# A chain of ten swiglu layers: each weight transfer of gate and up carries all eight feature chunks of one matrix instead of four chunks of both

## The chip, the core and the metric

One core of one Trainium2 chip runs the whole program. TensorE (PE) multiplies, ScalarE (ACT) and VectorE (DVE) work elementwise, and SyncE's queue (SP) starts every weight transfer. The metric is the device time of one execution in microseconds (us), lower is better.

## The reference, cut to what matters

Three model blocks follow each other on 256 tokens of width 1024, in float32. They hold ten swiglu layers, which the change touches, with mixers (delta rule, latent attention, state space, gating, pooling) between them:

```python
D_MODEL, SEQ, D_FF = 1024, 256, 2816
def swiglu(x, w_gu, w_down):
    gate, up = jnp.split(x @ w_gu, 2, axis=-1)
    return (jax.nn.silu(gate) * up) @ w_down
...
x = x + 0.5 * swiglu(rms_norm(x, ffn1_norm[l]), ffn1_w_gu[l], ffn1_w_down[l])
```

Eight of the ten layers normalize their input with a learned gain; two (in the second block) have no gain and no root mean square ahead of them.

## The kernel before

Every product is made of three float32r passes: a weight tile is split into a rounded part (`weights_hi`) and a rest (`weights_lo`), the input likewise (`input_hi`, `input_lo`), and TensorE adds hi x hi, hi x lo and lo x hi. Weights come as **items** of up to 1 MB. The plan of all items is written once, in order (`plan_ffn`, `plan_columns`, `plan_rows`), and five slots of SBUF hold them in turn. For each item, SP loads the raw weights into a slot once TensorE has used the item five places earlier (`load_weights`, L186); ACT rounds them (`round_weights`, L198), with the gain of each chunk of 128 features as its scale, so that an item with a gain takes one instruction for each chunk (L210) and one without takes one in all (L206); DVE writes the rest over the raw weights (`split_weights`, L215; L228 with a gain, L223 without). ACT and DVE are at most `LEAD` = 3 items ahead of TensorE. They run in order, and DVE starts an item after ACT has finished all of it.

A swiglu layer (`ffn`, L791) walks the 2816 hidden features in 11 steps of 256. In step s TensorE takes item a(s), which holds feature chunks 0 to 3 of the gate's 256 columns and of up's 256 columns, then item b(s) with chunks 4 to 7 of both, then the 256 rows of the down matrix of step s-1. So it goes gate, up, gate, up, 24 matmuls each, and then 24 wide ones. ACT and DVE in step s: round and split a(s)+3, scale the gate (L895), round and split b(s)+3, silu (L873), hidden = silu x up (L903), rounded hidden (L878), rest of it (L906), and round and split the item three places past the down item.

The last two down items are taken by `last_rows` (L292) in quarters of the output, so that the residual sum (L323, L325) and the transposes for the next layer's input (`turn`, L352; L360) can start before the end. Quarters come "by halves": the first two hold features 0 to 511 (chunks 0 to 3) of all tokens, the last two hold 512 to 1023 (chunks 4 to 7). ACT and DVE turn each into `input_hi` (L370) and `input_lo` (L385). In the first step `before_chunk` (L445) makes TensorE wait for the quarters that a chunk needs, and `sum_row` (L426, L430) sums the row of inverse roots that L895 multiplies with.

Between stages that are not joined stands a barrier (L150): all engines end their stage before any starts the next.

Of the kernel before, what the change touches and what calls it, by code (L numbers as in the profile page):

```python
# [13 lines left out]
P = 128  # L14
D = 1024
T = 256
NT = T // P
DC = D // P
FF = 2816
FSTEP = 256  # L20
# [72 lines left out]
class Core:  # L93
# [78 lines left out]

    def halves(self, gate, up, g0, u0, k0, gain):
        parts = [(slice(j * FSTEP, (j + 1) * FSTEP), w[k0 * P:(k0 + 4) * P, c0:c0 + FSTEP].rearrange("(k p) n -> p k n", p=P))
                 for j, (w, c0) in enumerate(((gate, g0), (up, u0)))]
        self.items.append((parts, 4, 2 * FSTEP, None if gain is None else (gain, k0)))
# [450 lines left out]
def plan_ffn(K, gate, up, g0, u0, down, gain):  # L627
    for s in range(NF):
        for k0 in (0, 4):
            K.halves(gate, up, g0 + s * FSTEP, u0 + s * FSTEP, k0, gain)  # L630
        if s:
            K.rows(down, (s - 1) * FSTEP, 2)
    K.rows(down, (NF - 1) * FSTEP, 2)
# [157 lines left out]
def ffn(K, feed, tail, alpha=1.0, join=True):  # L791
    nc, norm = K.nc, feed.norm
    gated, gscaled, silued, hidden, hrounded, hsplit = (K.count_of(s) for s in (
        "gate_ready", "gate_scaled", "gate_silued", "hidden_ready", "hidden_rounded", "hidden_split"))
    LAST = NF - 1
    with ExitStack() as e:
# [4 lines left out]
        with K.stage(3 * NF, join=join) as (block, n0):  # L801
# [14 lines left out]
            def _(pe):  # L816
                def part(bank, n, c0, w0, before=None):
                    wh, wl = K.item(n)
                    for m in range(2):
                        o, ms = bank[:, m * T:(m + 1) * T], slice(w0 + m * P, w0 + (m + 1) * P)  # L820
                        for k in range(4):
                            if before and m == 0:
                                before(pe, c0 + k)
                            c = c0 + k
                            nc.tensor.matmul(o, wh[:, k, ms], K.hi[:, c, :], start=(c == 0 and m == 0), stop=False,  # L825
                                             skip_group_check=True)
                            nc.tensor.matmul(o, wh[:, k, ms], K.lo[:, c, :], start=False, stop=False, skip_group_check=True)  # L827
                            last = nc.tensor.matmul(o, wl[:, k, ms], K.hi[:, c, :], start=False, stop=(c == DC - 1),  # L828
                                                    skip_group_check=True)
                    return last  # L830

# [1626 lines left out]
```

## Time and profile before

| what | before |
|---|---|
| median of 3 runs | 3296.45 us (3295.63 to 3297.97) |
| the profiled execution, its time and span | 3295.09 us, 3293.3 us |
| TensorE matmuls busy | 2952.7 us, 90% |
| DVE, ACT busy | 1847.4 us (56%), 1441.7 us (44%) |
| granted TensorE clock over the span | 0.931 |

Busy matmuls overlap, so 90% is not the share of peak. What decides is where TensorE stands still, and what it then waits for.

### The profile page before, as it was taken

The numbers are of one execution on the slowest core, as the hardware profiler recorded it, in microseconds if no ns is written. First come the engines' busy times: TensorE is split into PE (matmuls) and PEld (weight loads), VectorE is DVE, ScalarE is ACT, GpSimd is POOL, SyncE is SP. The second block draws the span as 40 slices with busy tenths as digits, with TensorE's granted clock in tenths as the row PEclk, the third lists the DMA queues.
The fourth block names the chain that finished last, engine by engine and source line by source line (L and its number), as shares of the span: only waits on it lengthen the run. The fifth ranks groups of instructions, "written<-read, shape, count | busy, mean of one in ns | idle before, by whom it ended". The sixth has DMA issues, their size and how long they took to land. (4 is left out here: it accounts for less than half of the span.)

```text
span 3293.3 us, 48031 instructions
## 1 busy us (share of the span) xinstructions
PE 2952.7 (90%) x20618; PEld 2734.3 (83%) x20618; DVE 1847.4 (56%) x2513; ACT 1441.7 (44%) x1925; POOL 16.3 (0%) x21
## 2 busy tenths in 40 slices
PE   4998788996997999999897698999999799999799
PEld 4998686996995699898797597898999699999698
DVE  3558464654554565545557635556554565655655
ACT  3544212544443454443434343344444354544543
POOL 0000000000000000000000100000000000000000
PEclk8999786998997899999998798999999899999899
DMA  4554100553552255555254043554555355554454
GB/s 160 180 191 155 64 1 26 185 188 112 179 190 94 71 192 192 168 191 165 91 167 143 1 154 117 177 192 154 192 185 161 123 183 192 179 192 141 167 189 138
DMA packets 371959, 489.30 MB, mean 149 GB/s; under 512 B 17103, under 2 KB 331044, under 8 KB 371620
## 3 DMA queue, kind: packets, MB, share of 16 engines
q1 hardware_dynamic: 371410, 486.11, 45.5%
q8 instruction: 163, 2.67, 0.3%
q14 instruction: 48, 0.39, 0.0%
q10 hardware_dynamic: 338, 0.13, 0.0%
HBM read 485.14 MB, written 1.05 MB: 148 GB/s over the span
## 5 line engine op out<-in xcount | busy, mean ns | idle before, releaser
L825 PE MATMUL work<-input_hi,weights_hi 128*128 128x256 f32 x3520 | 989.4, 281 | 8.8 <-PEq L150 6.8
L827 PE MATMUL work<-input_lo,weights_hi 128*128 128x256 f32 x3520 | 986.2, 280 | 0.0
L828 PE MATMUL work<-input_hi,weights_lo 128*128 128x256 f32 x3520 | 985.8, 280 | 0.0
L223 DVE TENSOR_TENSOR weights_lo<-weights_raw,weights_hi 128x2048 fp32r<-128x2048 f32 (+2 forms) x282 | 629.3, 2236 | 451.6 <-ACT weights_hi L206 451.3
L825 PEld LDWEIGHTS work<-input_hi,weights_hi 128*128 128x128 f32 x3520 | 666.6, 189 | 13.7 <-DVE weights_lo L228 6.9
L827 PEld LDWEIGHTS work<-input_lo,weights_hi 128*128 128x128 f32 x3520 | 666.9, 189 | 3.7
L828 PEld LDWEIGHTS work<-input_hi,weights_lo 128*128 128x128 f32 x3520 | 666.4, 189 | 0.0
L210 ACT ACTIVATE weights_hi<-weights_raw,params 128x512 fp32r<-128x512 f32 (+1 forms) x736 | 462.1, 701 | 363.8 <-DMA weights_raw<-in_ffn_w_in 177.0
L228 DVE SCALAR_TENSOR_TENSOR weights_lo<-weights_raw,params,weights_hi 128x512 fp32r<-128x512 f32 (+1 forms) x736 | 493.1, 733 | 224.7 <-ACT weights_hi L210 224.6
L206 ACT ACTIVATE weights_hi<-weights_raw 128x2048 fp32r<-128x2048 f32 (+2 forms) x282 | 524.6, 1862 | 173.0 <-DMA weights_raw<-in_ffn_w_up 106.2
L253 PE MATMUL work<-input_hi,weights_hi 128*128 128x256 f32 (+2 forms) x1160 | 333.2, 287 | 42.4 <-PEq L150 26.5
L286 PE MATMUL acc<-weights_hi,hidden_hi 128*128 128x512 f32 x880 | 344.7, 392 | 1.0 <-DVE hidden_lo L906 1.0
L287 PE MATMUL acc<-weights_lo,hidden_hi 128*128 128x512 f32 x880 | 343.6, 390 | 0.0
L288 PE MATMUL acc<-weights_hi,hidden_lo 128*128 128x512 f32 x880 | 342.7, 389 | 0.0
L254 PE MATMUL work<-input_lo,weights_hi 128*128 128x256 f32 (+2 forms) x1160 | 329.2, 284 | 0.0
L255 PE MATMUL work<-input_hi,weights_lo 128*128 128x256 f32 (+2 forms) x1160 | 329.1, 284 | 0.0
L253 PEld LDWEIGHTS work<-input_hi,weights_hi 128*128 128x128 f32 (+2 forms) x1160 | 221.5, 191 | 45.2 <-issue 41.9
L254 PEld LDWEIGHTS work<-input_lo,weights_hi 128*128 128x128 f32 (+2 forms) x1160 | 221.6, 191 | 0.7
L255 PEld LDWEIGHTS work<-input_hi,weights_lo 128*128 128x128 f32 (+2 forms) x1160 | 221.3, 191 | 0.5
L878 ACT ACTIVATE hidden_hi<-hidden 128x512 fp32r<-128x512 f32 x110 | 69.5, 632 | 292.7 <-DVE hidden L903 292.7
L895 DVE TENSOR_TENSOR gate_r<-work,inverse_root 128x512 f32<-128x512 f32 x88 | 60.8, 690 | 241.5 <-PE work L828 241.5
L288 PEld LDWEIGHTS acc<-weights_hi,hidden_lo 128*128 128x128 f32 x880 | 165.2, 188 | 35.5
(407 smaller groups left out, 3239.3 us busy)
## 6 DMA issues: line engine op xcount, KB each, us to landing
weights_raw<-in_ffn_w_gu SPq DMA_DIRECT2D x176, 512.0 KB, 4.7
weights_raw<-in_ffn_w_in SPq DMA_DIRECT2D x176, 512.0 KB, 4.6
weights_raw<-in_ffn_w_down SPq DMA_DIRECT2D x66, 1024.0 KB, 4.9
weights_raw<-in_w_in SPq DMA_DIRECT2D x44, 1024.0 KB, 5.1
weights_raw<-in_ffn_w_out SPq DMA_DIRECT2D x44, 1024.0 KB, 4.8
weights_raw<-in_a_w_in SPq DMA_DIRECT2D x29, 1024.0 KB, 5.5
weights_raw<-in_ffn_w_gate SPq DMA_DIRECT2D x44, 512.0 KB, 3.7
weights_raw<-in_ffn_w_up SPq DMA_DIRECT2D x44, 512.0 KB, 4.7
```

What stands on the lines that cost most here:

```text
L206: last = self.nc.scalar.activation(self.wh[:, n % SLOTS, 0:kc * cols], raw, ACT.Copy)
L210: last = self.nc.scalar.activation(hi[:, k, :], raw[:, k * cols:(k + 1) * cols], ACT.Copy, scale=g[:, gain[1] + k:gain[1] + k + 1])
L223: last = self.nc.vector.tensor_tensor(self.wl[:, n % SLOTS, 0:kc * cols], raw, self.wh[:, n % SLOTS, 0:kc * cols].bitcast(F32), ALU.subtract)
L228: last = self.nc.vector.scalar_tensor_tensor(out=lo[:, k, :], in0=raw[:, k * cols:(k + 1) * cols], scalar=g[:, gain[1] + k:gain[1] + k + 1 ...
L253: self.nc.tensor.matmul(o, wh[:, k, ms], hi[:, k, :], start=clear, stop=False, skip_group_check=True)
L254: self.nc.tensor.matmul(o, wh[:, k, ms], lo[:, k, :], start=False, stop=False, skip_group_check=True)
L255: last = self.nc.tensor.matmul(o, wl[:, k, ms], hi[:, k, :], start=False, stop=(k == kc - 1), skip_group_check=True)
L286: self.nc.tensor.matmul(o, hi[:, k, ts], wh[:, k, cols], start=(first and k == 0), stop=False, skip_group_check=True)
L288: last = self.nc.tensor.matmul(o, lo[:, k, ts], wh[:, k, cols], start=False, stop=(end and k == kc - 1), skip_group_check=True)
L825: nc.tensor.matmul(o, wh[:, k, ms], K.hi[:, c, :], start=(c == 0 and m == 0), stop=False, skip_group_check=True)
L827: nc.tensor.matmul(o, wh[:, k, ms], K.lo[:, c, :], start=False, stop=False, skip_group_check=True)
L828: last = nc.tensor.matmul(o, wl[:, k, ms], K.hi[:, c, :], start=False, stop=(c == DC - 1), skip_group_check=True)
```

## The change

An item of gate or up now holds all eight chunks of the 256 columns of one matrix, [128, 8, 256], in one transfer. Before, it held four chunks of both matrices, [128, 4, 512], in two transfers. Item a(s) is the gate's and item b(s) is up's. The number and size of items stay as they are. TensorE uses the helper `project` (L237), which takes an item's 48 matmuls; given `before`, it takes chunks 0 to 3 of both column halves and then chunks 4 to 7. The semaphore `gate_ready` goes; its waiters now wait until item a(s) is used.

```diff
-    def halves(self, gate, up, g0, u0, k0, gain):
-        parts = [(slice(j * FSTEP, (j + 1) * FSTEP), w[k0 * P:(k0 + 4) * P, c0:c0 + FSTEP].rearrange("(k p) n -> p k n", p=P))
-                 for j, (w, c0) in enumerate(((gate, g0), (up, u0)))]
-        self.items.append((parts, 4, 2 * FSTEP, None if gain is None else (gain, k0)))
...
     for s in range(NF):
-        for k0 in (0, 4):
-            K.halves(gate, up, g0 + s * FSTEP, u0 + s * FSTEP, k0, gain)
+        for w, c0 in ((gate, g0), (up, u0)):
+            K.columns(w, c0 + s * FSTEP, FSTEP, DC, gain)
...
                 for s in range(NF):
-                    before = feed.before_chunk if s == 0 else None
-                    K.arrived(pe, a_item(s))
                     if s >= 2:
                         pe.wait_ge(*(gscaled if norm else silued)(s - 1))
-                    part(gate_bank(s), a_item(s), 0, 0, before)
+                    K.project(pe, a_item(s), gate_bank(s), (K.hi, K.lo),
+                              (lambda k: feed.before_chunk(pe, k)) if s == 0 else None)
+                    if s == 0:
+                        feed.sum_row(pe)
                     if s >= 2:
                         pe.wait_ge(*hidden(s - 1))
-                    part(up_bank(s), a_item(s), 0, FSTEP).then_inc(K.used, 1)
-                    if s == 0:
-                        feed.sum_row(pe)
-                    K.arrived(pe, b_item(s))
-                    part(gate_bank(s), b_item(s), 4, 0, before).then_inc(*gated.up())
-                    part(up_bank(s), b_item(s), 4, FSTEP).then_inc(K.used, 1)
+                    K.project(pe, b_item(s), up_bank(s), (K.hi, K.lo))
...
-                        act.wait_ge(*gated(s + 1))
+                        act.wait_ge(K.used, a_item(s) + 1)
...
-                        dve.wait_ge(*gated(s + 1))
+                        dve.wait_ge(K.used, a_item(s) + 1)
```

On ACT, this is the stage of the latent keys, just ahead of the barrier to the third swiglu layer, whose first three items are rounded there; before:

```order
L210 ACTIVATE weights_hi<-weights_raw,params 128x512 x4
L1888 ACTIVATE k_nope<-work 128x512
L1891 ACTIVATE v_mla<-work 128x2x256
L210 ACTIVATE weights_hi<-weights_raw,params 128x512 x4
L1888 ACTIVATE k_nope<-work 128x512
L1891 ACTIVATE v_mla<-work 128x2x256
L210 ACTIVATE weights_hi<-weights_raw,params 128x512 x4
L150 UNCONDITIONAL_BRANCH
```

and with the change:

```order
L205 ACTIVATE weights_hi<-weights_raw,params 128x256 x8
L1864 ACTIVATE k_nope<-work 128x512
L1867 ACTIVATE v_mla<-work 128x2x256
L205 ACTIVATE weights_hi<-weights_raw,params 128x256 x8
L1864 ACTIVATE k_nope<-work 128x512
L1867 ACTIVATE v_mla<-work 128x2x256
L205 ACTIVATE weights_hi<-weights_raw,params 128x256 x8
L150 UNCONDITIONAL_BRANCH
```

The order is the same, and each of the three items takes eight instructions of 256 columns where it took four of 512.

On DVE, this is the end of the output projection ahead of the second swiglu layer: the last weight split, then the residual sums (L325) that the transposes wait for. Before:

```order
L603 TENSOR_TENSOR input_lo<-h,input_hi 128x256 x8
L223 TENSOR_TENSOR weights_lo<-weights_raw,weights_hi 128x2048
L228 SCALAR_TENSOR_TENSOR weights_lo<-weights_raw,params,weights_hi 128x512 x8
L325 SCALAR_TENSOR_TENSOR x<-x,acc 128x512 x2
L385 TENSOR_TENSOR input_lo<-work,input_hi 128x4x128 x2
L325 SCALAR_TENSOR_TENSOR x<-x,acc 128x512 x2
```

and with the change (L320 is the same sum):

```order
L598 TENSOR_TENSOR input_lo<-h,input_hi 128x256 x8
L218 TENSOR_TENSOR weights_lo<-weights_raw,weights_hi 128x2048
L223 SCALAR_TENSOR_TENSOR weights_lo<-weights_raw,params,weights_hi 128x256 x16
L320 SCALAR_TENSOR_TENSOR x<-x,acc 128x512 x2
L380 TENSOR_TENSOR input_lo<-work,input_hi 128x4x128 x2
L320 SCALAR_TENSOR_TENSOR x<-x,acc 128x512 x2
```

Here too the order is kept, and sixteen short instructions stand ahead of the sums in place of eight.

On TensorE, this is the first step of the second swiglu layer; rows show the semaphores waited for. Before, chunk 4 comes only with item b:

```order
L825 MATMUL work<-input_hi,weights_hi 128x256
L827 MATMUL work<-input_lo,weights_hi 128x256
L828 MATMUL work<-input_hi,weights_lo 128x256
L430 MATMUL acc<-root_diagonals,const 128x256 [waits input_diagonal]
L825 MATMUL work<-input_hi,weights_hi 128x256 [waits input_split,weights_split]
L827 MATMUL work<-input_lo,weights_hi 128x256
```

and with the change, the wait for the second half of the input stands 24 matmuls earlier, in the middle of item a:

```order
L248 MATMUL work<-input_hi,weights_hi 128x256
L249 MATMUL work<-input_lo,weights_hi 128x256
L250 MATMUL work<-input_hi,weights_lo 128x256
L248 MATMUL work<-input_hi,weights_hi 128x256 [waits input_split]
L249 MATMUL work<-input_lo,weights_hi 128x256
L250 MATMUL work<-input_hi,weights_lo 128x256
```

The wait for `input_split` that stood with item b's first matmul, behind 48 matmuls, now stands behind 24.

## Rows read from the trace of the kernel before

**Rows 1.** Windows, first of eight steady stretches: time, PE, PEld, DVE, ACT, clock; and their sum.

```profile
107.00:240.00 133.00, 133.00 (x960) 125.40 (x959) 77.81 (x97) 65.51 (x88) 0.00 (x0) 1.00 0.59 190
...
sum 969.00, PE 969.00 PEld 912.47 DVE 561.44 ACT 476.83 POOL 0.00; mean PE 121.12 PEld 114.06 DVE 70.18 ACT 59.60 POOL 0.00
```

**Rows 2.** Groups by line and shape, the whole trace: the weight instructions of ACT and DVE.

```profile
L210 ACT ACTIVATE weights_hi<-weights_raw,params 128x512 fp32r<-128x512 f32 x704 | 450.2, 712 | 355.7 <-DMA weights_raw<-in_ffn_w_in 177.0 <-DMA weights_raw<-in_ffn_w_gu 175.7 <-PEq L150 3.1
...
L228 DVE SCALAR_TENSOR_TENSOR weights_lo<-weights_raw,params,weights_hi 128x512 fp32r<-128x512 f32 x704 | 481.7, 747 | 224.7 <-ACT weights_hi L210 224.6
```

**Rows 3.** Timeline (start, us): items of eight 128x256 pieces, latent key projection.

```profile
750.20 3.31 ACT L210 ACTIVATE weights_hi<-weights_raw,params 128x256 fp32r<-128x256 f32 x8 [4.29 <-DMA weights_raw<-in_w_dkv]
...
753.55 3.26 DVE L228 SCALAR_TENSOR_TENSOR weights_lo<-weights_raw,params,weights_hi 128x256 fp32r<-128x256 f32 x8
```

**Rows 4.** Timeline of ACT and DVE, one steady step of layer 3.

```profile
851.16 2.56 ACT L210 ACTIVATE weights_hi<-weights_raw,params 128x512 fp32r<-128x512 f32 x4 [2.30 <-DMA weights_raw<-in_ffn_w_gu]
...
856.16 2.57 ACT L210 ACTIVATE weights_hi<-weights_raw,params 128x512 fp32r<-128x512 f32 x4 [2.44 <-DMA weights_raw<-in_ffn_w_gu]
...
862.40 0.68 DVE L903 TENSOR_TENSOR hidden<-silu,work 128x512 f32<-128x512 f32 x1
...
879.06 0.68 DVE L903 TENSOR_TENSOR hidden<-silu,work 128x512 f32<-128x512 f32 x1
```

**Rows 5.** Timeline around the barrier ahead of the memory values.

```profile
47.51 2.54 ACT L210 ACTIVATE weights_hi<-weights_raw,params 128x512 fp32r<-128x512 f32 x4
...
50.09 2.74 DVE L228 SCALAR_TENSOR_TENSOR weights_lo<-weights_raw,params,weights_hi 128x512 fp32r<-128x512 f32 x4 [3.14 <-ACT weights_hi L210]
...
53.15 0.55 PE L1116 MATMUL work<-weights_hi,input_hi 128*128 128x256 f32 x1 [6.93 <-PEq L150]
```

**Rows 6.** Timeline around the barrier ahead of the first layer's input.

```profile
69.43 2.74 DVE L228 SCALAR_TENSOR_TENSOR weights_lo<-weights_raw,params,weights_hi 128x512 fp32r<-128x512 f32 x4 [2.93 <-ACT weights_hi L210]
...
72.88 0.45 PE L360 MATMUL work<-const,x 128*128 128x128 f32 x1 [6.80 <-PEq L150]
```

**Rows 7.** Timeline around the barrier ahead of layer 3.

```profile
810.05 0.60 ACT L1888 ACTIVATE k_nope<-work 128x512 f32<-128x512 f32 x1 [0.58 <-PE work L1875]
...
814.17 0.60 ACT L1888 ACTIVATE k_nope<-work 128x512 f32<-128x512 f32 x1 [0.60 <-PE work L1875]
...
815.14 2.55 ACT L210 ACTIVATE weights_hi<-weights_raw,params 128x512 fp32r<-128x512 f32 x4
...
817.72 2.74 DVE L228 SCALAR_TENSOR_TENSOR weights_lo<-weights_raw,params,weights_hi 128x512 fp32r<-128x512 f32 x4 [1.37 <-ACT weights_hi L210]
...
820.96 0.55 PE L825 MATMUL work<-input_hi,weights_hi 128*128 128x256 f32 x1 [6.83 <-PEq L150]
```

**Rows 8.** Timeline, end of the output projection ahead of layer 2.

```profile
571.86 2.74 DVE L228 SCALAR_TENSOR_TENSOR weights_lo<-weights_raw,params,weights_hi 128x512 fp32r<-128x512 f32 x4 [7.10 <-ACT weights_hi L210]
...
574.63 1.28 DVE L325 SCALAR_TENSOR_TENSOR x<-x,acc 128x512 f32<-128x512 f32 x2
...
576.27 0.60 PE L360 MATMUL work<-const,x 128*128 128x128 f32 x4
```

**Rows 9.** Timeline, first step of layer 2: last quarter's split, and a later matmul.

```profile
583.74 0.69 DVE L385 TENSOR_TENSOR input_lo<-work,input_hi 128x512 fp32r<-128x512 f32 x1 [0.45 <-ACT input_hi L370]
...
585.02 0.28 PE L825 MATMUL work<-input_hi,weights_hi 128*128 128x256 f32 x1
```

**Rows 10.** Page, part 6: issues, KB each, median us to landing.

```profile
weights_raw<-in_ffn_w_in SPq DMA_DIRECT2D x176, 512.0 KB, 4.6
...
weights_raw<-in_w_in SPq DMA_DIRECT2D x44, 1024.0 KB, 5.1
```

**Rows 11.** Waits of TensorE within layers, whole trace, and one in time.

```profile
PE work L825 <- DVE input_lo L385: 2.0, 3, 0.7
...
758.94 0.47 PE L286 MATMUL acc<-weights_hi,hidden_hi 128*128 128x512 f32 x1 [0.52 <-DVE hidden_lo L906]
```

**Rows 12.** Window behind the barrier ahead of layer 3: granted clock before the DMA share.

```profile
820.90:827.00 6.10, 6.04 (x39) 6.07 (x40) 2.74 (x4) 5.50 (x6) 0.00 (x0) 0.73 0.00 0
```

More of the change, by code:

```diff
@@ L792, in ffn @@
     nc, norm = K.nc, feed.norm
-    gated, gscaled, silued, hidden, hrounded, hsplit = (K.count_of(s) for s in (
-        "gate_ready", "gate_scaled", "gate_silued", "hidden_ready", "hidden_rounded", "hidden_split"))
+    gscaled, silued, hidden, hrounded, hsplit = (K.count_of(s) for s in (
+        "gate_scaled", "gate_silued", "hidden_ready", "hidden_rounded", "hidden_split"))
     LAST = NF - 1
@@ L816, in _ @@
             def _(pe):
[L817 to L830, printed above, removed]
                 def pair(s):
```

## Prediction

> **What bounds the kernel now.** I read first the windows of steady stretches inside the swiglu layers, to see whether TensorE ever stands still there. It does not: in eight such stretches of 969 us together its matmuls cover all 969 us and the granted clock is 1.00, while DVE is busy for 561 us (58%) and ACT for 477 us (49%) [rows 1]. One step takes 879.06 - 862.40 = 16.66 us [rows 4]. So inside the layers TensorE's own 120 matmuls a step set the time, and their number, shapes and operands do not change. Then I read the list of TensorE's waits, to see where it stands still elsewhere: at barriers between stages, and at transposes and inputs. A change of the weight items can only act there, or by making ACT and DVE so slow that they fall behind in the steps.
>
> **The cost of an item on ACT and DVE.** The trace already has the new form: in the latent key projection an item with a gain is eight pieces of 256 columns, and takes 3.31 us on ACT and 3.26 us on DVE [rows 3], against 2.56 and 2.74 us for four pieces of 512 [rows 4, 5]. That is +0.75 us on ACT and +0.52 us on DVE for each item. The eight layers with a gain have 704 / 4 = 176 such items [rows 2]: ACT gets 132 us more work, DVE 92 us. The two layers without a gain take one instruction for each item in either form, so 44 items stay as they are.
>
> The Trainium skill ("VectorE: DVE Perf Modes", the section on the TRN2 errata) says that operations from SBUF pay a fixed extra cost for each instruction and advises tiles of at least 512 elements; the change goes from 512 to 256. The trace agrees on the direction. By the page's ScalarE figure of 224 cycles at 1.2 GHz, four more instructions cost 0.75 us, an estimate that is equal to the row; the sum would be the same. The page does not say whether the cost is hidden; that is decided below.
>
> **Inside a step it is hidden.** ACT's first weight item of a step began at 851.16 because its transfer had landed then, and the second at 856.16 for the same reason [rows 4]. With 3.31 us each ACT ends at 854.5 and 859.5, DVE ends the second at 859.5 + 3.3 = 862.8, and the hidden product starts there instead of at 862.40, 0.4 us later. TensorE asks for the result a whole step later, after the next up product. The longest chain of the two engines in a step is: first round 3.3, its split 3.3 and the scaled gate 0.7 (beside the second round), second split 3.3, hidden 0.7, its rounding 0.6, and the round of the down item 1.9, 13.8 us of 16.66. So it does not build up: price 0. If that cover were gone, each microsecond over 16.66 would count 80 times or so. The gate is complete after 48 matmuls of a step instead of 72, so DVE's scaling can come 2.8 us sooner; nobody on the path waits for it, price 0.
>
> **Where it is not hidden: three barriers.** At three places ACT rounds and DVE splits an item of a coming layer as the last act of a stage, and the barrier lets TensorE go only behind it.
> - Ahead of the memory values ACT starts at 47.51, DVE at 50.09 and ends at 52.83, and TensorE starts at 53.15 after 6.93 us of idle time at the barrier [rows 5]. No transfer is waited for. Cost: 0.75 + 0.52 = 1.27 us.
> - Ahead of the first layer's input DVE ends at 72.17 and TensorE starts at 72.88, again after 6.80 us [rows 6]. Cost: 1.27 us.
> - Ahead of layer 3 three items are rounded in turn with the copies of k_nope and v_mla between. ACT idled 0.58 and 0.60 us ahead of the second and third copy, which takes up part: 3 x 0.75 - 0.58 - 0.60 = 1.07 us, and DVE's last split adds 0.52. DVE's end goes from 820.46 to 822.05, and TensorE's start at 820.96 follows [rows 7]. Cost: 1.6 us.
> Together 4.1 us. Lower bound 0, if something else than DVE holds the barriers; upper bound 4.1 plus what the clock does (below).
>
> **Four ends of output projections.** There DVE splits the second item of the next layer and then does the residual sums for the first transposes. Ahead of layer 2 the split at 571.86 was DVE's wait for ACT, and the sums start right behind it at 574.63; the first is done after half of 1.28 us, at 575.3, and TensorE transposes at 576.27 [rows 8], 0.96 us of room. The split moves by 1.27 us, so the transpose is late by about 0.3 us. Ahead of layers 4, 8 and 10 the pattern is the same, with slightly more room: I take 0.9 us for the four, bounds 0 and 4 x 0.35 = 1.4.
>
> **The earlier wait for the second half of the input.** In the first step TensorE needed features 512 to 1023 after 48 matmuls, and now needs them after 24. Layer 2's last quarter is split at 583.74 + 0.69 = 584.43, and the 25th matmul starts at 585.02 [rows 9]: 0.6 us to spare. ACT's and DVE's work between the last transpose and that split is not weight work, so it moves along with TensorE. The whole trace has only 2.0 us of TensorE's waits for this input in the layers, three of them [rows 11]. Price 0.
>
> **Transfers.** 440 issues of 512 KB become 220 of 1024 KB, with the same 1 KB runs. A half lands 4.6 us after its own issue, and the second is issued behind the first; a single 1024 KB item of just the new shape (in_w_in) lands in 5.1 us [rows 10], 0.5 us more, which the dropped second issue about makes up. Price 0, bounds -0.5 to +0.4 us a transfer, which ACT's waits inside the steps take up.
>
> **Ends of layers.** At the end of two layers TensorE waited about half a microsecond for the rest of the last hidden product (0.52 us at 758.94) [rows 11]. The earlier gate can give back up to 1.0 us of that, and slower splits can add up to 0.5 us at others; I take 0.
>
> **The sum** is 4.1 + 0.9 = 5.0 us. The profiled execution took 3295.09 us, so 3300.1 us for one like it; the median of the runs shown is 1.4 us above it, and I predict 3296.45 + 5.0 = 3301.4 us, 0.15% more. Changes within 0.2% (6.6 us, up to 3303.0) are about what a measurement cannot tell from no change, and the forecast lies there, near the edge.
>
> **The rivals.**
> - Slower by more than 0.2%, by the clock. The three barriers' idle times grow from 6.9 to about 8.3 us. Behind the barrier ahead of layer 3 the granted clock averages 0.73 over 6.1 us [rows 12]: 3.3 us at 1.2 GHz, or 1.65 us lost. If each of the three low stretches doubled, 3 x 1.65 = 5 us come on top: 3306. For it: these stretches exist. Against it: they depend on how the start falls, and may as well shorten. Chance 0.15; it decides from 1.6 us of added cost on.
> - Slower by the second half of the input: if the last quarter were more than 0.6 us later, five starts (layers 2, 4, 8, 9, 10) each lose the excess, for 1.3 us of delay 0.7 us each, 3.5 us: 3305. Against it: the quarter hangs on TensorE's transposes, not on weights, except in layer 9. Chance 0.1.
> - Much slower: ACT and DVE fall behind in the steps of 16.66 us, because some wait that I take as loose is tight. One microsecond in each of 80 steps would give 3380. Rows 1 and the 13.8 us speak against it. Chance 0.04.
> - Not slower at all: something other than DVE's split ends the barriers, or transfers land earlier and give the 0.9 us back. Then 3296.5 to 3297.5. Chance 0.13.
> - Faster by more than 0.2%: fuller transfers speed up the whole. TensorE would need 6.6 us of waits for weights inside the layers to win; apart from the barriers, the rows have 2.0 us for inputs and about 1.0 for the hidden product [rows 11]. Chance 0.04. The Trainium skill ("DMA: Bandwidth & Descriptors", the rules for kernel authors) advises transfers of at least 1 MB, which speaks for this one; by that rule alone, with nobody waiting, the time would stay at 3296.5.
> - My forecast, 3298.5 to 3303.5: chance 0.54.
>
> **Range and chances.** 3296.5 to 3306.5 leaves out the far case and the ends of the clock's. Slower by over 0.2%: the clock 0.13, the input 0.09, the far case 0.04 and the forecast's own upper edge 0.06, 0.32 together. Faster by over 0.2%: 0.04. Within: 0.64.
>
> **What would show it.** In the profile after: ACT's and DVE's weight groups at 1408 pieces with a mean near 0.5 us; ACT busy 1574 us, DVE 1939 us; TensorE's three starts behind the barriers 1.3, 2.5 and (with the transposes ahead of layer 2) about 4.5 us later than before; steady windows with TensorE at 100%; a step still 16.66 us; no wait for `input_lo` near the 25th matmul. The prediction is wrong if steps are longer than 16.7 us, if the starts do not move, or if the low-clock stretches change in length.

## The result and the profile after

| | before | after |
|---|---|---|
| median of 20 runs each | 3296.32 us (3292.25 to 3298.87) | 3303.08 us (3296.61 to 3308.07) |
| ratio after / before | | 1.002, 95% interval 1.0013 to 1.0027 |
| profiled execution, its time and span | 3295.09 us, 3293.3 us | 3301.61 us, 3299.8 us |
| TensorE matmuls busy | 2952.7 us | 2953.4 us |
| DVE, ACT busy | 1847.4, 1441.7 us | 1937.0, 1562.4 us |

The change costs 0.2%, 4.3 to 8.9 us by the interval, at the edge of what can be told from no change. The forecast was +5.0 us, 3301.4 us. The median rose by 6.8 us. Between the two profiled executions the span grew by 6.5 us. ACT got 120.7 us more work and DVE 89.6 us, and TensorE, which has the longest list of work, is busy for the same time.

The page after, its busy times, two costly groups and two of the issues (they answer to [rows 2] and [rows 10]; the groups here hold 32 pieces that are not of gate and up):

```profile
PE 2953.4 (90%) x20618; PEld 2734.9 (83%) x20618; DVE 1937.0 (59%) x3217; ACT 1562.4 (47%) x2629; POOL 16.7 (1%) x21
...
L223 DVE SCALAR_TENSOR_TENSOR weights_lo<-weights_raw,params,weights_hi 128x256 fp32r<-128x256 f32 x1440 | 584.6, 478 | 360.2 <-ACT weights_hi L205 360.2
L205 ACT ACTIVATE weights_hi<-weights_raw,params 128x256 fp32r<-128x256 f32 x1440 | 592.8, 495 | 263.8 <-DMA weights_raw<-in_ffn_w_in 128.1
...
weights_raw<-in_ffn_w_gu SPq DMA_DIRECT2D x88, 1024.0 KB, 5.1
weights_raw<-in_w_in SPq DMA_DIRECT2D x44, 1024.0 KB, 5.2
```

A piece takes half a microsecond where one of twice the size took 0.71 to 0.75, so ACT and DVE pay for twice as many instructions. Inside the layers nobody notices. Windows after (columns as in [rows 1]) and, behind them, two hidden products of layer 3 on DVE that are four steps apart:

```profile
107.00:240.00 133.00, 133.00 (x960) 125.40 (x959) 88.88 (x168) 76.98 (x154) 0.00 (x0) 1.00 0.58 190
860.00:980.00 120.00, 120.00 (x871) 113.28 (x871) 77.17 (x146) 68.05 (x137) 0.00 (x0) 1.00 0.59 192
```

```profile
869.73 0.68 DVE L879 TENSOR_TENSOR hidden<-silu,work 128x512 f32<-128x512 f32 x1
...
936.35 0.69 DVE L879 TENSOR_TENSOR hidden<-silu,work 128x512 f32<-128x512 f32 x1
```

TensorE is covered to 100% at a granted clock of 1.00, with DVE at 88.88 us of 133 where it had 77.81, and a step takes (936.35 - 869.73) / 4 = 16.66 us as before. The time is lost at single places. TensorE's rows behind the three barriers, timeline after, to be laid beside [rows 5 to 7]:

```profile
54.64 0.55 PE L1092 MATMUL work<-weights_hi,input_hi 128*128 128x256 f32 x1 [8.19 <-PEq L150]
...
76.68 1.94 PE L355 MATMUL work<-const,x 128*128 128x128 f32 x8 [8.06 <-PEq L150]
...
828.59 0.55 PE L248 MATMUL work<-input_hi,weights_hi 128*128 128x256 f32 x1 [8.11 <-PEq L150]
```

The idle times were 6.93, 6.80 and 6.83 us: +1.26, +1.26 and +1.28, 3.8 us together. I then laid TensorE's instructions of both traces side by side, in their order, and looked where the distance between equal instructions changes. Besides the barriers it does so in two ways.

One is waits. At the end of layer 2 TensorE waits 0.20 us for the hidden product where it waited 0.52 [rows 11]. At the end of layer 3 and in the output projection of the pool mixer ahead of layer 10 it waits longer. After:

```profile
997.99 2.11 ACT L205 ACTIVATE weights_hi<-weights_raw,params 128x256 fp32r<-128x256 f32 x5 [5.50 <-DMA weights_raw<-in_b_w_in]
...
1006.72 0.47 PE L281 MATMUL acc<-weights_hi,hidden_hi 128*128 128x512 f32 x1 [1.45 <-DVE hidden_lo L882]
...
3075.88 1.91 ACT L201 ACTIVATE weights_hi<-weights_raw 128x2048 fp32r<-128x2048 f32 x1 [1.45 <-DMA weights_raw<-in_b_w_out]
...
3081.95 0.80 PE L281 MATMUL acc<-weights_hi,input_hi 128*128 128x512 f32 x1 [10.64 <-DVE input_lo L598]
```

The two waits of TensorE were 0.48 and 8.79 us before, so +0.97 and +1.85 us. Each time ACT had stood waiting for a transfer that the change does not touch (`in_b_w_in`, `in_b_w_out`).

The traces of the experiments e1 to e11, which the next section tells one by one, set these two places apart. At the end of layer 3 the long wait comes back in each of the two other traces that have the changed items and their short instructions in all steps: 1.69 us in e3 and 1.47 in e4. Their transfer of `in_b_w_in` landed 6.85 and 6.63 us after its issue, and 6.61 in the changed kernel. The wait is 0.48 to 0.49 us in the kernel before, e1, e5, e6 and e7, and 0.00 to 0.29 us in e2, e9, e10 and e11, and in all nine the transfer landed after 5.0 to 5.5 us. (In e8, with instructions of 128 columns, it is 2.44 us with a landing of 5.1.) So this 1 us belongs to the change, although why the transfer lands later is open. At the pool mixer the wait goes from 8.69 to 9.82 us in the seven traces with the old items and from 9.30 to 10.67 in the four with new ones in all steps. The ranges overlap, so one pair of traces cannot say how much of the 1.85 us is the change's.

The other way is the clock. The same two matmuls of the latent keys' stage, ahead of the third barrier, before and then after:

```profile
804.17 0.27 PE L1874 MATMUL work<-weights_lo,latent_hi 128*128 128x128 f32 x1
...
807.72 0.28 PE L1875 MATMUL work<-weights_hi,latent_lo 128*128 128x128 f32 x1
```

```profile
807.22 0.41 PE L1850 MATMUL work<-weights_lo,latent_hi 128*128 128x128 f32 x1
...
813.83 0.41 PE L1851 MATMUL work<-weights_hi,latent_lo 128*128 128x128 f32 x1
```

They are 3.55 us apart before and 6.61 us after, and over the whole stage the trace after loses 3.8 us. Windows over that stage (column 8 is the granted clock), before and after:

```profile
796.00:823.00 27.00, 17.37 (x119) 16.43 (x120) 10.15 (x17) 13.53 (x24) 0.00 (x0) 0.75 0.36 118
```

```profile
798.00:831.00 33.00, 21.51 (x121) 20.61 (x122) 11.69 (x29) 15.98 (x39) 0.00 (x0) 0.60 0.29 96
```

A mean of 0.75 over 27 us is 13.5 us at 1.2 GHz, 0.60 over 33 us is 26.4 us. Between 1030 and 1953 us of the trace before, the trace after wins 4.3 us back, all but 0.5 us of it without a shorter wait. Over the whole span the granted clock is 0.931 and 0.930.

Behind the first barrier the clock is lower, too. The 15 us from TensorE's start, before and then after:

```profile
53.15:68.15 15.00, 12.93 (x96) 12.73 (x96) 2.74 (x4) 5.31 (x11) 0.00 (x0) 0.90 0.28 81
```

```profile
54.64:69.64 15.00, 13.99 (x96) 13.79 (x96) 2.59 (x7) 5.00 (x13) 0.00 (x0) 0.82 0.22 70
```

The same 96 matmuls take about 1.0 us more. This repeats: in the four traces in which TensorE idles 8.19 us at that barrier (after, e1, e3, e6) these 15 us have 0.80 to 0.82, in the three with 6.93 us (before, e2, e7) 0.89 to 0.90, and in the three with 1.70 us (e4, e5, e11) 1.00. With 5.83 us (e9, e10) it is 0.86. Behind the second barrier the clock is 0.76 before and after, and behind the third 0.89 and 0.91.

### The profile page after: what moved, and what is told of

Same layout as the page of the kernel before. It is cut to its first block and busy times, and to the rows that moved or that the text cites. A ratio compares the mean times of both kernels' runs of the same rounds, so it can differ in the third digit from the quotient of the medians.

```text
span 3299.8 us, 49309 instructions
## 1 busy us (share of the span) xinstructions
PE 2953.4 (90%) x20618; PEld 2734.9 (83%) x20618; DVE 1937.0 (59%) x3217; ACT 1562.4 (47%) x2629; POOL 16.7 (1%) x21
## 5 line engine op out<-in xcount | busy, mean ns | idle before, releaser
L248 PE MATMUL work<-input_hi,weights_hi 128*128 128x256 f32 (+1 forms) x4680 | 1321.7, 282 | 52.5 <-PEq L150 34.6
L249 PE MATMUL work<-input_lo,weights_hi 128*128 128x256 f32 (+1 forms) x4680 | 1314.6, 281 | 0.0
L250 PE MATMUL work<-input_hi,weights_lo 128*128 128x256 f32 (+1 forms) x4680 | 1313.9, 281 | 0.0
L248 PEld LDWEIGHTS work<-input_hi,weights_hi 128*128 128x128 f32 (+1 forms) x4680 | 887.7, 190 | 59.9 <-issue 41.7
L249 PEld LDWEIGHTS work<-input_lo,weights_hi 128*128 128x128 f32 (+1 forms) x4680 | 887.9, 190 | 4.3
L250 PEld LDWEIGHTS work<-input_hi,weights_lo 128*128 128x128 f32 (+1 forms) x4680 | 887.2, 190 | 0.4
L223 DVE SCALAR_TENSOR_TENSOR weights_lo<-weights_raw,params,weights_hi 128x256 fp32r<-128x256 f32 x1440 | 584.6, 478 | 360.2 <-ACT weights_hi L205 360.2
L205 ACT ACTIVATE weights_hi<-weights_raw,params 128x256 fp32r<-128x256 f32 x1440 | 592.8, 495 | 263.8 <-DMA weights_raw<-in_ffn_w_in 128.1
L281 PEld LDWEIGHTS acc<-weights_hi,hidden_hi 128*128 128x128 f32 x880 | 165.3, 188 | 34.5 <-issue 3.3
L282 PEld LDWEIGHTS acc<-weights_lo,hidden_hi 128*128 128x128 f32 x880 | 165.2, 188 | 30.2
L1092 PE MATMUL work<-weights_hi,input_hi 128*128 128x256 f32 x224 | 65.9, 294 | 19.1 <-PEq L150 19.1
```

What stands on the lines that cost most here:

```text
L205: last = self.nc.scalar.activation(hi[:, k, :], raw[:, k * cols:(k + 1) * cols], ACT.Copy, scale=g[:, gain[1] + k:gain[1] + k + 1])
L223: last = self.nc.vector.scalar_tensor_tensor(out=lo[:, k, :], in0=raw[:, k * cols:(k + 1) * cols], scalar=g[:, gain[1] + k:gain[1] + k + 1 ...
L248: self.nc.tensor.matmul(o, wh[:, k, ms], hi[:, k, :], start=clear, stop=False, skip_group_check=True)
L249: self.nc.tensor.matmul(o, wh[:, k, ms], lo[:, k, :], start=False, stop=False, skip_group_check=True)
L250: last = self.nc.tensor.matmul(o, wl[:, k, ms], hi[:, k, :], start=False, stop=(k == kc - 1), skip_group_check=True)
L281: self.nc.tensor.matmul(o, hi[:, k, ts], wh[:, k, cols], start=(first and k == 0), stop=False, skip_group_check=True)
```

## The experiments

Every kernel was timed in rounds with the kernel before on the same chip, and the ratio is to that.

| kernel | median, us | ratio (95%) |
|---|---|---|
| e1 short instructions alone | 3306.19 | 1.0032 (1.002 to 1.0043) |
| e2 first two steps in the old form | 3296.15 | 1.0002 (0.9993 to 1.0011) |
| e3 two transfers for each item | 3301.20 | 1.0017 (1.0009 to 1.0026) |
| e4 change, with hold | 3283.40 | 0.9962 (0.9948 to 0.9976) |
| e5 before, with hold | 3276.88 | 0.9947 (0.9933 to 0.996) |
| e6 five items ahead of barriers | 3303.99 | 1.0023 (1.0013 to 1.0032) |
| e7 items at projections, 128 columns | 3310.82 | 1.0045 (1.0032 to 1.0058) |
| e8 all items, 128 columns | 3385.35 | 1.0277 (1.0259 to 1.0295) |
| e9 before, one instruction an item | 3296.62 | 1.0003 (0.9994 to 1.0012) |
| e10 after, one instruction an item | 3298.08 | 1.0007 (0.9998 to 1.0016) |
| e11 mixed items, with hold | 3281.75 | 0.9954 (0.9941 to 0.9967) |

The median of the kernel before was 3297.34 us beside e1 to e4, 3295.17 beside e5 to e8 and 3296.29 beside e9 to e11.

**Short instructions or new transfers (e1, e3).** e1 is the kernel before with the pieces cut in two, on ACT and likewise on DVE:

```diff
-                    last = self.nc.scalar.activation(hi[:, k, :], raw[:, k * cols:(k + 1) * cols], ACT.Copy,
-                                                     scale=g[:, gain[1] + k:gain[1] + k + 1])
+                    for c in range(0, cols, 256):
+                        e = min(c + 256, cols)
+                        last = self.nc.scalar.activation(hi[:, k, c:e], raw[:, k * cols + c:k * cols + e], ACT.Copy,
+                                                         scale=g[:, gain[1] + k:gain[1] + k + 1])
```

> The kernel before, items, transfers and TensorE's order unchanged; only ACT and DVE take each item with a gain in eight pieces of 256 columns instead of four of 512. Theory 1 (the cost is the 0.75 us of ACT and 0.52 us of DVE that each item takes longer, where a barrier or a transpose waits for it): +4.1 us at the three barriers and about +0.9 at the four projections, 3301 to 3303 us, as the changed kernel. Rival 2 (single transfers of 1024 KB or the landing of items cost the time): nothing, 3296 us. Rival 3 (gate first, then up, with the earlier wait for the second half of the input costs it): nothing, 3296 us.

e3 is the changed kernel with two transfers of four chunks each:

```diff
-                sp.dma_start(self.raw_item(n).rearrange("p (k n) -> p k n", k=kc)[:, :, cols], src).then_inc(*landed.up(16))
+                dst = self.raw_item(n).rearrange("p (k n) -> p k n", k=kc)[:, :, cols]
+                for k0 in ((0, 4) if n in self.two else (0,)):
+                    ks = slice(k0, k0 + 4) if n in self.two else slice(0, kc)
+                    sp.dma_start(dst[:, ks, :], src[:, ks, :]).then_inc(*landed.up(16))
```

> The changed kernel, but each item of gate and up is loaded by two transfers of 512 KB (chunks 0 to 3, then 4 to 7). Theory 1: the transfers are not on the path, 3303 us as the changed kernel. Rival 2 (the single transfer lands later or disturbs others): back to 3297 us or half of the way.

e1 loses 0.32% with the transfers and TensorE's order of before; e3 loses what the change loses. The number of instructions is enough for the loss, and one transfer or two makes no difference to the total that these runs can tell. e1's time of 3306.19 us is above its expected 3301 to 3303, and its ratio gives 10.5 us. Its trace has the three barriers (+3.8 us) and the four projections (+1.1 us) as expected, and besides them an attention stage behind layer 3 at a low clock, like e6 below.

**Which items (e2, e6, e7).** e2 is the changed kernel, but the items of steps 0 and 1 of each layer are four chunks of both matrices again (`halves` for `s < 2`), with TensorE's order of before in these steps.

> The changed kernel, but steps 0 and 1 of every swiglu layer keep the old items (four chunks of both matrices) and the old order; steps 2 to 10 are as changed. Theory 1: all places where the items' longer work is exposed handle items of steps 0 and 1 alone, so the loss goes, 3296 to 3297.5 us. Rival 2 (transfers): 9 of 11 steps still have single transfers, so about 9/11 of the loss stays, 3301.8 us. Rival 3 (order): the early wait for the input lies in step 0 and goes too, 3296 us, with e1 telling it from theory 1.

The loss is gone, with nine of eleven steps in the new form, and in its trace the idle times at the barriers are back at 6.93, 6.80 and 6.80 us. e2 restores instructions, transfers and order of the first two steps together; that it is the instructions follows from e1. e6 goes the other way, with 256-column pieces for five items alone:

```diff
+            if (gain, s, k0) in (("ffn1_0", 0, 0), ("ffn1_0", 1, 0), ("ffn1_1", 0, 0), ("ffn1_1", 0, 4), ("ffn1_1", 1, 0)):
+                K.short.add(len(K.items) - 1)
```

> The kernel before, with smaller instructions of 256 columns (eight where there were four) on five items alone: the two of layer 1 and the three of layer 3 that stand ahead of the three barriers. All other items, the transfers and TensorE's order stay. Theory: three barriers late by 1.3, 1.3 and 1.6 us, 4.1 to 4.5 us together, 3301.5, with the clock's stretches adding or taking up to 2 us. Rival (the loss is spread over all layers, or comes from the gate's order): within 1 us of the kernel before, 3297 to 3298.

TensorE behind the three barriers in e6:

```profile
54.59 0.55 PE L1126 MATMUL work<-weights_hi,input_hi 128*128 128x256 f32 x1 [8.19 <-PEq L150]
...
76.62 1.94 PE L368 MATMUL work<-const,x 128*128 128x128 f32 x8 [8.05 <-PEq L150]
...
826.07 0.55 PE L835 MATMUL work<-input_hi,weights_hi 128*128 128x256 f32 x1 [8.14 <-PEq L150]
```

The three idle times are those of the changed kernel to 0.03 us. These 20 more instructions on each of two engines cost as much at the barriers as 704 do. But the total was 7.6 us by the ratio (4.3 to 10.5), not 4.1 to 4.5. In the attention behind layer 3 the windows of before and of e6 show where its trace lost the most besides, by the clock:

```profile
1080.00:1116.00 36.00, 29.45 (x116) 18.74 (x116) 23.02 (x63) 16.63 (x46) 0.00 (x0) 0.83 0.00 1
```

```profile
1085.00:1128.00 43.00, 37.42 (x118) 23.18 (x118) 23.11 (x63) 16.14 (x46) 0.00 (x0) 0.66 0.00 1
```

The same work takes about 7 us more at a mean clock of 0.66; 5.7 us come back between 1110 and 1950 us of the trace before. e7 puts pieces of 128 columns on the first three items of layers 2, 4, 8 and 10, which stand at the ends of projections.

> The kernel before, with the first three items of layers 2, 4, 8 and 10 in instructions of 128 columns (sixteen where there were four): ACT takes 2.2 us more for each, DVE 1.6 us. This is three times the dose of the change, at the ends of the four projections alone. Theory (the splits there stand ahead of the residual sums, with 0.96 us of room): the second split ends 3.8 us later or more, and the transposes come 2.8 us late or more at each of the four places, 11 us together or more: 3308 to 3315. If the loss there is linear and has no room at all, the change itself would have cost more than 1 us at each of the four. Rival (the sums were waiting for TensorE's quarters anyway, so the splits are covered): under 3 us, 3297 to 3300.

```profile
579.43 0.90 PE L368 MATMUL work<-const,x 128*128 128x128 f32 x3 [2.74 <-DVE x L333]
```

That is layer 2's first transpose in e7 (idle before it in brackets); the three others wait 2.72, 2.72 and 2.70 us. Predicted was 3.8 - 0.96 = 2.8. Four times 2.72 are 10.9 us, and by the ratio the time rose by 14.8 us (10.5 to 19.1), again more than the waits, as in e6. The room of 0.96 us is real. Whether the change itself uses it up is seen in e1 and after. The transfers, ACT's item, DVE's sum and the transpose, first in e1 and then in the changed kernel:

```profile
566.26 16.00 SPq L194 DMA_DIRECT2D weights_raw<-in_ffn_w_gu  x6
571.89 3.31 ACT L212 ACTIVATE weights_hi<-weights_raw,params 128x256 fp32r<-128x256 f32 x8 [5.22 <-DMA weights_raw<-in_ffn_w_gu]
578.52 1.29 DVE L330 SCALAR_TENSOR_TENSOR x<-x,acc 128x512 f32<-128x512 f32 x2
579.27 0.66 PE L365 MATMUL work<-const,x 128*128 128x128 f32 x4 [0.44 <-DVE x L330]
```

```profile
566.11 14.94 SPq L189 DMA_DIRECT2D weights_raw<-in_ffn_w_gu  x3
571.21 3.31 ACT L205 ACTIVATE weights_hi<-weights_raw,params 128x256 fp32r<-128x256 f32 x8 [4.70 <-DMA weights_raw<-in_ffn_w_gu]
577.84 1.28 DVE L320 SCALAR_TENSOR_TENSOR x<-x,acc 128x512 f32<-128x512 f32 x2
578.59 0.65 PE L355 MATMUL work<-const,x 128*128 128x128 f32 x4
```

In e1 ACT has the item 571.89 - 566.26 = 5.63 us after the first issue, and the transpose waits 0.44 us. In the changed kernel it has it after 5.10 us, and the transpose does not wait. It is not the single transfer that does this. e3 has the new item in two transfers of 512 KB:

```profile
567.08 15.44 SPq L192 DMA_DIRECT2D weights_raw<-in_ffn_w_gu  x6
572.15 3.31 ACT L208 ACTIVATE weights_hi<-weights_raw,params 128x256 fp32r<-128x256 f32 x8 [4.65 <-DMA weights_raw<-in_ffn_w_gu]
...
579.52 0.66 PE L358 MATMUL work<-const,x 128*128 128x128 f32 x4
```

The item is there after 5.07 us, and TensorE waits at none of the four projections. Over all items of gate and up, the median time from the first issue to the last landing is 5.08 us in the changed kernel and 5.08 in e3, against 5.36 to 5.43 in the kernels with the old items (before, e1, e5, e6, e7, e9). The item that holds one matrix lands sooner, in one transfer or in two. Why is open.

**Dose inside the steps (e8).** Pieces of 128 columns for every item with a gain, by the edit of e1.

> The kernel before, with every item that has a gain in instructions of 128 columns, sixteen where there were four (the change made it eight). ACT about 4.8 us for an item, DVE 4.3 us. Theory (inside a step the smaller instructions are hidden only while the chain of ACT and DVE is under the 16.66 us of TensorE; 13.8 us with the change): the chain comes to 17.4 us, so steps of the eight layers with a gain take 17 to 18 us and some 80 of them cost 0.5 to 1 us each, on top of 12 us at the barriers and 11 us at the projections' ends: 3350 to 3400. Rival (the order of ACT and DVE has more slack than that chain, and only their busy time of about 14 us a step counts): steps stay at 16.66 us, and only the barriers and ends cost, 3315 to 3325.

Two hidden products in neighbouring steps of layer 3, and TensorE's waits (total, times, longest) in e8:

```profile
942.99 0.68 DVE L908 TENSOR_TENSOR hidden<-silu,work 128x512 f32<-128x512 f32 x1
959.87 0.69 DVE L908 TENSOR_TENSOR hidden<-silu,work 128x512 f32<-128x512 f32 x1
```

```profile
PE acc L291 <- DVE hidden_lo L911: 32.0, 9, 6.5
...
PE work L365 <- DVE x L330: 11.2, 4, 3.0
```

The step is 16.89 us, 0.23 us over the 16.66 of TensorE, in nearly every step of the eight layers with a gain. The time of 3385 us lies in the expected range, but it is put together otherwise. The 11.2 us at the four projections and 3 x 3.8 us at the barriers, whose idle times are 10.71, 10.57 and 10.60, are as expected. The steps cost some 80 x 0.23 = 18 us, where 40 to 80 were expected. Another 32.0 us are nine waits for the last hidden product at the ends of layers, up to 6.5 us each (two of 0.5 us before), and were not expected. About 19 us are left, for which the estimate of the clock's share below gives 28.

**The barriers without the item (e4, e5, e11).** The last item ahead of each barrier is held back and rounded right behind it:

```diff
-        upto = min(upto, self.taken + LEAD)
+        upto = min(upto, self.taken + LEAD, self.limit)
...
+                K.round_weights(act, n0 + LEAD)
...
+        K.limit = K.taken + NH // 2 + 2
...
+        K.limit = 1 << 20
```

> The changed kernel, but at the three barriers the last item is not rounded and split ahead of the barrier: it is held back for the next stage. Theory 1: TensorE's idle times at the three barriers (8.2, 8.1 and 8.1 us) fall, to what ACT's copies leave, some 2 us at the first two and 4 at the third, so 3303 - 16 = 3287 us, and the difference to the kernel before with the same edit should be near 2 us. If something else than DVE's split holds the barriers: 3303 us.

> The kernel before, with the last item ahead of each of the three barriers held back and rounded only behind it, as in e4_hold_after. Theory (DVE's split of that item sets the barriers, and the smaller instructions cost the changed kernel its time there and at the projections' ends): the hold takes the same work from both kernels, so the kernel before gains nearly what the changed one gained less what the change had put on the three barriers. From 3297.3 it comes to 3282 to 3285, and the difference between the two held kernels is within 3 us of zero, where it was 6.8 us unheld. TensorE's three idle times of 6.9, 6.8 and 6.8 us at the barriers fall by at least 2.5 us each. Rival (the loss sits elsewhere, in steps or transfers, and the hold gives a gain of its own): the difference of 5 to 7 us stays, so the held kernel before takes 3276 to 3278.

> The changed kernel with the hold of e4_hold_after at the three barriers and the first two steps of each layer in the old item form, as in e2_hybrid2: in all other steps gate and up are items of one matrix. Theory (barriers and the first steps' items hold all of the loss): as fast as the held kernel before, e5_hold_before, ratio to the kernel before 0.993 to 0.996, 3275 to 3284. Rival (something else in the changed steps costs, too): as e4_hold_after or slower, ratio 0.996 to 0.998, above 3283.

TensorE behind the barriers, e5 and then e4:

```profile
47.32 0.36 PE L1117 MATMUL work<-weights_hi,input_hi 128*128 128x256 f32 x1 [1.70 <-PEq L150]
...
60.63 1.07 PE L360 MATMUL work<-const,x 128*128 128x128 f32 x8 [1.71 <-PEq L150]
...
802.09 0.38 PE L825 MATMUL work<-input_hi,weights_hi 128*128 128x256 f32 x1 [2.69 <-PEq L150]
```

```profile
48.37 0.36 PE L1093 MATMUL work<-weights_hi,input_hi 128*128 128x256 f32 x1 [1.70 <-PEq L150]
...
62.35 1.07 PE L355 MATMUL work<-const,x 128*128 128x128 f32 x8 [2.39 <-PEq L150]
...
810.94 0.55 PE L248 MATMUL work<-input_hi,weights_hi 128*128 128x256 f32 x1 [3.95 <-PEq L150]
```

The idle time falls to 1.7 us at the first barrier in both, by 5.2 and 6.5 us, about the time of that item on ACT and DVE together (5.3 and 6.6 us): DVE's split of the waiting item did hold the barriers. The held kernels beat both originals, e5 by 0.53%. e5 missed its expectation: it took 3276.88 us, below the 3282 to 3285 of the theory and inside the rival's 3276 to 3278. e4 was 3.6 us faster than its 3287. The difference between e4 and e5 is 0.15%, 5 us, with an uncertainty of about 6 us, so the medians leave open whether the hold removes the change's loss or keeps it. In the traces 0.0 + 0.68 + 1.26 = 1.9 us of the barriers' 3.8 us is left, since at the third one an earlier short item still stands in line, and the waits at the end of layer 3 (1.47 against 0.49 us) remain. e11 took 3281.75 us, in the theory's range, but it lies between e4 and e5, and its executions spread over 11 us, so it decides nothing. e5's three idle times are 14.5 us shorter together, and by the ratio its time is 17.5 us shorter (13.2 to 22.1).

**Everything but the instructions (e9, e10).** In `round_weights` and `split_weights`, `if gain is None:` became `if True:`, in the kernel before and in the changed one, which leaves the gains out.

> The kernel before, but no item of weights is multiplied by its gain, so that each is rounded by one instruction of 2048 columns (1.92 us) and split by one (2.29 us), as items without a gain are; the learned gains of eight layers are left out of the result. Three barriers come 1.1 us earlier each: 3 to 4 us less than the kernel before. Both theories expect the same here; it is the base for e10_after_one_instruction.

> The changed kernel with the same omission: one instruction of 2048 columns for each item, the learned gains left out. Transfers of 1024 KB, the order of gate and up on TensorE and the waits on the gate are those of the changed kernel. Theory (the change costs only by its shorter instructions): within 2 us of e9_before_one_instruction. Rival (the transfers or the order of gate and up cost something by themselves, as at the two places late in the trace where an item landed later): 3 to 7 us above e9.

TensorE behind the first and second barrier in e9, and in e10:

```profile
52.27 0.55 PE L1116 MATMUL work<-weights_hi,input_hi 128*128 128x256 f32 x1 [5.83 <-PEq L150]
...
71.45 1.94 PE L360 MATMUL work<-const,x 128*128 128x128 f32 x8 [5.71 <-PEq L150]
```

```profile
52.20 0.55 PE L1092 MATMUL work<-weights_hi,input_hi 128*128 128x256 f32 x1 [5.83 <-PEq L150]
...
71.44 1.94 PE L355 MATMUL work<-const,x 128*128 128x128 f32 x8 [5.70 <-PEq L150]
```

The two lie 1.5 us apart in the median, with an uncertainty of about 4 us, and their traces nowhere more than 0.7 us from each other. With the instruction count made equal, one transfer or two, the order of gate and up and the earlier need of the input's second half are worth nothing that can be measured by themselves. That does not clear them together with short instructions: the wait of 1.45 us at the end of layer 3 is 0.48 with short instructions alone (e1) and 0.00 with the new items and order alone (e10).

e9 also missed an expectation: its three idle times fell by 1.1 us each, as worked out, but its median equals that of before. Its trace loses about 7 us in the latent keys' stage, between matmuls that stand at 803 and 812 us of the trace before, in a low-clock stretch like that of the changed kernel. This execution is the slowest of e9's eleven, so why the median did not fall stays open.

**The clock's share.** Span x (1 - mean clock) of an execution is an estimate of what the low clock costs, if TensorE's work fills the span. Its mean is 232.2 us over the 20 executions of the changed kernel, and 230.6, 228.0 and 228.7 over the 57 of the kernel before beside the experiments: 1.6 to 4.3 us more with the change. For e1 it is 6.2 us more than for the kernel before beside it, for e6 7.1, for e7 3.0, for e8 27.6 and for e9 0.4. What the waits leave open is 5.6, 3.8 and 3.9 us in e1, e6 and e7, so the clock is large enough for it. The estimate is coarse: idle time at the low clock counts in it too, and for e10 it gives 5.0 us, where the median is 1.8 us above the kernel before.

## Why the prediction was right, point by point

The range and the place of the main loss were right. The total came as near as it did partly by luck, since terms that did not happen and losses that the sum did not have nearly cancel.

- **Bound, and cost of an item.** Right. ACT was predicted at 1574 us and measured at 1562.4, DVE at 1939 and 1937.0. A piece takes 495 and 478 ns on average over the trace.
- **Hidden inside a step, price 0.** Right: 16.66 us and 100%. e8 shows how much of the cover is left: counted like the 13.8 us of the prediction, its chain comes to 17.4 us, and its step takes 16.89, so the chain was counted some 0.5 us too long. But e8 also shows that the waits for the last hidden product at the ends of layers (32 us) cost more than the steps (18 us).
- **Three barriers, 4.1 us.** Right: idle +1.26, +1.26 and +1.28, 3.8 us. At the third I took 1.6 us. Measured against the matmuls just ahead of the barrier it moved by 1.5, of which 1.28 are idle time. e6 made the same three numbers with five items; e8, e9 and e10 moved all three by what was added to or taken from the item there, and e4 and e5 the first by the whole item.
- **Projections' ends, 0.9 us.** Right for the old items (0.44, 0.22, 0.30 and 0.13 us in the transposes of layers 2, 4, 8 and 10 in e1, 1.1 us together), wrong for the change: no transpose waits. The new item lands 0.3 to 0.5 us sooner, which was the favourable bound of the transfers' term, and I had priced that at 0. Its reason there, the dropped second issue, was wrong as well: e3 keeps both issues and lands as soon. The term is 0.
- **Second half of the input.** Right, there is no new wait, and e10 against e9 confirms it.
- **Ends of layers, 0.** -0.32 at layer 2, +0.97 at layer 3, whose loss is larger than the bound of 0.5. It comes back in e3 and e4, so it is the change's. That term took landing times as fixed, and the transfer of the next stage's first item, whose rounding and splitting the last hidden product stands behind, landed 1.4 us later.
- **Not in the sum at all.** The wait ahead of the pool mixer's output projection, +1.85 us. Its cause was not settled. The transfer that is late there is the same in both kernels, and in e9, with the transfers of before, the wait was 9.82 us, in e1 8.89 us. So it varies with the execution, and the form of the new transfers is not needed for it. At 2050 us another projection's wait fell from 7.57 to 7.23 us. It is 7.23 in the three traces with one transfer for each item (after, e4, e10) and at least 7.57 in all others, e3 among them: SP's second issue, 0.4 us behind the first, stands there ahead of a stage, which starts 0.34 us later with it.
- **The clock.** I gave the rival 0.15 on the thought that low stretches behind the barriers double. One of the three grew, that behind the first barrier, by 1.0 us and in all four traces with that idle time. The large one lies in the stage of the latent keys, ahead of the third barrier, and cost 3.8 us; 1.5 us near 560 us and most of 4.3 us between 1030 and 1953 us came back. The net is near 1 us in this pair of traces, and 1.6 to 4.3 us by the estimate over the executions.
- **The signs.** The pieces, the busy times, the steady windows and the step came as said. TensorE's three starts were to be 1.3, 2.5 and 4.5 us later and were 1.5, 3.8 and 7.6 us later. Waits account for 1.3, 2.5 and 3.5 us of that; the rest came without a wait, nearly all of it where the clock was lower. Low-clock stretches that change in length were named as a sign of being wrong, and they did change.

The sum of what the pair shows is 3.8 barriers, -0.3 + 1.0 ends of layers, 1.85 pool mixer and -0.3 at 2050 us, 6.0 us of the 6.5. All idle times ahead of TensorE's matmuls together grew by 5.7 us, which leaves 0.8 us for the clock's net. The prediction's 5.0 us were 3.8 at its place, and 1.2 us (0.9 and the larger barrier term) that did not happen, made up by 2.2 us of waits that it had not. What stays open is how much of the median's 6.8 us is the clock's beyond that estimate.

## What to carry to other kernels

Twice as many instructions of half the size, on engines that are half idle, cost nothing in the steady steps here and their full price at each place where such an item is the last thing ahead of a barrier: count these places and multiply by one item. This gives the idle time. The total can rise by more, since low-clock stretches change with it: e6 rose by 7.6 us for 3.8 us of idle time at the barriers. The cheap remedy is the order: the item that no one needs yet goes behind the barrier, which gave 0.53% here, more than the choice of item form. Half as many transfers of twice the size were worth 0.3 us at one place, where the second issue held up the start of a stage, and nothing elsewhere. Where two kernels differ in two ways, as e1 and the change do in transfers and item form, only a run that changes one of them (e3) tells which one counts.

## What the runs showed of the hardware

- The granted clock's low stretches lie differently in nearly equal kernels. In the stage of the latent keys the mean clock was 0.75 before and 0.60 after, and in e9 0.55 over 32 us, with barriers 1.1 us shorter; in e6 the attention had 0.66 instead of 0.83. Single stretches are worth 3 to 7 us, as much as the whole change, and part of it returned within 900 us. Executions of one kernel spread by 6.6 us before and 11.5 us after.
- The 15 us behind the first barrier had a mean clock of 0.89 to 0.90 after 6.93 us of idle time on TensorE, 0.80 to 0.82 after 8.19 us, and 1.00 after 1.70 us (ten traces).
- The same untouched transfer of 1024 KB landed 5.0 to 5.5 us after its issue at the end of layer 3 in ten traces, and 6.6 to 6.9 us after it in the three with the new items and short instructions in all steps, with 1.0 us of it reaching TensorE.
- An item of eight chunks of one matrix was there 5.08 us (median) after its first issue, in one transfer of 1024 KB or in two of 512 KB, and an item of four chunks of two matrices, in two of 512 KB, after 5.36 to 5.43 us.
